# Early units of u beside the selection and between the expert matrix's steps, with the one-hot weights on ScalarE

## The reference, cut to what matters

```python
q = (xb @ w_q).reshape(tb, 8, 2, 128)
s = einsum('thpd,hpnd->thpn', q, sub_keys)          # 128 scores for each half key
sv, si = top_k(s, 16)
cand = (sv[:, :, 0, :, None] + sv[:, :, 1, None, :]).reshape(tb, 8, 256)
top_v, top_i = top_k(cand, 16)
experts = take_along_axis(cand_idx, top_i, -1)      # cand_idx = si[half 0] * 128 + si[half 1]
g = softmax(top_v)
a = gelu(einsum('td,thkd->thk', xb, u[experts]))
y = einsum('thk,thkd->td', g * a, v[experts])
```

## Time and profile before

| | |
|---|---|
| median of 3 runs | 1603.01 us (1602.9 to 1603.34) |
| profiled execution | 1604.01 us, its span 1602.2 us |
| mean granted TensorE clock | 0.953 |
| busy | PE 1429.9 us (89%), PEld 1287.4 (80%), DVE 939.9 (59%), ACT 711.7 (44%), POOL 564.4 (35%) |
| HBM | 259.85 MB read, 4.46 MB written |

### The profile page before, as it was taken

One profiled execution on the slowest core, in us unless ns is written; L12 is line 12 of the kernel. 1 busy time (PEld: TensorE's weight loads), 2 busy tenths in 40 slices (PEclk: granted clock), 3 DMA queues, 4 the chain that ended last, 5 costly groups with the idle time before them and its releaser, 6 DMA issues.

```text
span 1602.2 us, 21914 instructions
## 1 busy us (share of the span) xinstructions
PE 1429.9 (89%) x8932; PEld 1287.4 (80%) x8932; DVE 939.9 (59%) x1493; ACT 711.7 (44%) x991; POOL 564.4 (35%) x314
## 2 busy tenths in 40 slices
PE   6878878999997987977467799999999999999997
PEld 6767767999886766877466688999999999999996
DVE  4786677544455565799788655544444444444444
ACT  4544444544444454432222344544444444444442
POOL 2661012444354103677588721221212222121222
PEclk9999879999999999989788899999999999999999
DMA  8564335777774614534200066666555655555554
GB/s 269 157 187 128 110 116 189 250 234 247 238 242 135 204 59 134 173 95 142 82 1 1 21 201 196 209 190 191 185 188 190 188 186 188 191 185 188 191 187 171
DMA packets 183124, 265.74 MB, mean 166 GB/s; under 512 B 8384, under 2 KB 119744, under 8 KB 182768
## 3 DMA queue, kind: packets, MB, share of 16 engines
q1 hardware_dynamic: 182048, 261.47, 50.8%
q0 software_dynamic: 400, 1.25, 0.3%
q10 hardware_dynamic: 576, 1.63, 0.3%
HBM read 259.85 MB, written 4.46 MB: 165 GB/s over the span
## 4 chain that ended last, share of the span: by engine, by line
PE 70%; DVE 14%; POOL 7%; issue 3%; DMA 3%; ACT 2%; SPq 0%; DVEq 0%; POOLq 0%; ACTq 0%
PE bank L614 21%; PE bank L645 17%; PE bank L619 10%; PE bank L650 8%; POOL sb_hot L1951 5%; PE bank L587 4%; PE bank L591 2%; DVE sb_ada_junk L1260 2%; DMA sb_raw<-w_in 2%; PE bank L890 2%; DVE sb_hot L1761 1%; DVE sb_lo L1244 1%; PE bank L829 1%; PE bank L732 1%; PE bank L848 1%
## 5 line engine op out<-in xcount | busy, mean ns | idle before, releaser
L1812 POOL TENSOR_TENSOR sb_lo<-sb_raw,sb_hi 128x1024 fp32r<-128x1024 f32 (+1 forms) x152 | 373.9, 2467 | 904.3 <-ACT sb_hi L922 904.3
L922 ACT ACTIVATE sb_hi<-sb_raw 128x1024 fp32r<-128x1024 f32 (+2 forms) x427 | 444.5, 1048 | 402.0 <-DMA sb_raw<-peer_v 128.7
L1244 DVE TENSOR_TENSOR sb_lo<-sb_raw,sb_hi 128x1024 fp32r<-128x1024 f32 (+2 forms) x276 | 361.7, 1316 | 412.4 <-ACT sb_hi L922 411.8
L614 PE MATMUL bank<-sb_act_hi,sb_hi 128*128 128x256 f32 x1632 | 410.0, 288 | 5.2 <-ACT sb_hi L922 5.2
L614 PE MATMUL bank<-sb_act_lo,sb_hi 128*128 128x256 f32 x1632 | 407.1, 286 | 0.0
L614 PEld LDWEIGHTS bank<-sb_act_hi,sb_hi 128*128 128x128 f32 x1632 | 318.2, 195 | 9.1 <-issue 4.8
L614 PEld LDWEIGHTS bank<-sb_act_lo,sb_hi 128*128 128x128 f32 x1632 | 318.5, 195 | 2.7 <-issue 0.2
L619 PE MATMUL bank<-sb_act_hi,sb_lo 128*128 128x256 f32 x1632 | 233.0, 286 | 21.0 <-POOL sb_lo L1812 21.0
L645 PE MATMUL bank<-sb_hi,sb_hid_lo 128*128 128x512 f32 x600 | 234.3, 391 | 0.0
L645 PE MATMUL bank<-sb_hi,sb_hid_hi 128*128 128x512 f32 x600 | 234.1, 390 | 0.0
L619 PEld LDWEIGHTS bank<-sb_act_hi,sb_lo 128*128 128x128 f32 x1632 | 213.9, 195 | 22.4 <-POOL sb_lo L1812 22.4
(11 more groups left out here) (317 smaller groups left out, 1467.6 us busy)
## 6 DMA issues: line engine op xcount, KB each, us to landing
sb_raw<-peer_uT SPq DMA_DIRECT2D x128, 512.0 KB, 3.7
sb_raw<-peer_v SPq DMA_DIRECT2D x128, 512.0 KB, 3.6
sb_raw<-w_in SPq DMA_DIRECT2D x52, 512.0 KB, 4.4
sb_ada_w<-ada_wT SPq DMA_DIRECT2D x48, 512.0 KB, 5.0
sb_raw<-w_gate SPq DMA_DIRECT2D x22, 512.0 KB, 3.9
sb_raw<-w_up SPq DMA_DIRECT2D x22, 512.0 KB, 4.1
sb_raw<-w_down SPq DMA_DIRECT2D x22, 512.0 KB, 3.9
sb_raw<-w_out SPq DMA_DIRECT2D x16, 512.0 KB, 4.4
```

What stands on the lines that cost most here:

```text
L614: e.matmul(bank[:, j * T:(j + 1) * T], hi[:, k, j * P:(j + 1) * P], part[:, k0 + k, :], start=i == first_i and j == 0 and k == 0 and part ...
L922: e.activation(flat_of(i, "hi"), flat_of(i, "raw"), ACT.Copy).then_inc(hi_done[i % R], 1)
L1244: e.tensor_tensor(flat_of(i, "lo"), flat_of(i, "raw"), flat_of(i, "hi").bitcast(F32), ALU.subtract).then_inc(lo_done[i % R], 1)
L1812: e.tensor_tensor(flat_of(i, "lo"), flat_of(i, "raw"), flat_of(i, "hi").bitcast(F32), ALU.subtract).then_inc(lo_done[i % R], 1)
```

## The change

1. The selection computes 13 early units instead of 7 (`EARLY_BESIDE_SELECT`), in a new order. GpSimd's two small operations of a D are put off until the lo parts of the H or E that follows are done.
2. 19 further units (`EARLY_BESIDE_G`) are computed between the 64 steps of the expert matrix: `expert_matrix_order` gives one block of u, then one or two steps of G, 38 and 64 in all. Their lo parts are shared in halves by GpSimd and VectorE (`early_G=2`); VectorE is one block ahead with them, not three. So 32 units are early, and the sweep has 32 pairs: one unit of u and two of v.
3. The multiply by the weights leaves GpSimd. ScalarE does it as four `Copy` activations of 128x128 with the token's weight as scale. Its copies into G and its Gelus run five entries of the order later (`G_LATER`).
4. The store of an early unit is issued by ScalarE, right behind the Gelu, not by SyncE. The 19 units of the expert matrix use one more buffer, a fourth.

```diff
-SELECT_ORDER = "HDHHDHDHHDHDHEDEDEEDEDEE"
+SELECT_ORDER = "HDHHDHHDHHDHDEEDEEEDEEEDEEDEEE"
+EARLY_BESIDE_G = 19
+EARLY_BESIDE_SELECT = SELECT_ORDER.count("E")
+EARLY = EARLY_BESIDE_SELECT + EARLY_BESIDE_G
+HOT_BUFS = 3
+G_LATER = 5
+def expert_matrix_order():
+    n_blocks, q = 2 * EARLY_BESIDE_G, 0
+    for b in range(n_blocks):
+        yield "u", EARLY_BESIDE_SELECT + b // 2, b % 2
+        while q * n_blocks < (b + 1) * N_G:
+            yield "G", q, 0
+            q += 1
...
 # TensorE
-            for q in range(N_G):
-                bank = take("G", q)
-                pe.wait_ge(*hot_done.at(q))
+            for what, n, b in expert_matrix_order():
+                if what == "u":
+                    if b == 0:
+                        early_panel = feature_panel(("uT", n), act_T, h2)
+                    next(early_panel, None)
+                else:
+                    bank, h = take("G", n), hot[n % HOT_BUFS]
+                    pe.wait_ge(*hot_done.at(n))
...
 # ScalarE
+            def early_out(u):
+                b, nth = early_slot(u)
+                act.wait_ge(early_stored[b], 16 * nth)
+                act.wait_ge(*full(("uT", u)))
+                e.activation(by_chunk(early_buf[b]), by_chunk(psum(("uT", u))[:, :]), ACT.Gelu).then_inc(*gives(("uT", u)))
+                act.wait_ge(*freed(("uT", u)))
+                e.dma_start(parked_units[u], early_buf[b]).then_inc(early_stored[b], 16)
...
+            order = list(expert_matrix_order())
+            for at in range(len(order) + G_LATER):
+                if at < len(order) and order[at][0] == "u":
+                    hi_until(("uT", order[at][1]), order[at][2])
+                elif at < len(order):
+                    q = order[at][1]
+                    act.wait_ge(*hot_eq.at(q))
+                    for j in range(TG):
+                        h = hot[q % HOT_BUFS][:, 1, j, :]
+                        ins = e.activation(h, h, ACT.Copy, scale=pT[:, 2, q * TG + j:q * TG + j + 1])
+                    ins.then_inc(*hot_done.inc(q))
+                if at >= G_LATER:
+                    what, n, b = order[at - G_LATER]
+                    if what == "G":
+                        copy_out(Gv[:, :, n * TG:(n + 1) * TG], psum("G", n)[:, :].rearrange("p (t i) -> p i t", t=TG), "G", n)
+                    elif b == 1:
+                        early_out(n)
...
 # VectorE
+            for what, n, b in expert_matrix_order():
+                if what == "u":
+                    lo_until(("uT", n), b, 1)
+                else:
+                    h = hot[n % HOT_BUFS]
+                    if n >= HOT_BUFS:
+                        dve.wait_ge(*full("G", n - HOT_BUFS))
...
 # GpSimd
-            for q in range(N_G):
-                pool.wait_ge(*hot_eq.at(q))
-                h = hot[q % HID_BUFS][:, 1]
-                e.tensor_tensor(h, h, pT[:, 2, q * TG:(q + 1) * TG].unsqueeze(2).to_broadcast([P, TG, P]), ALU.mult).then_inc(*hot_done.inc(q))
+            for what, n, b in expert_matrix_order():
+                if what == "u":
+                    lo_until(("uT", n), b)
```

More of the change, by code:

```diff
@@ L67 @@
 SLOT = 2 * BLOCK
[L69 removed]
+POOL_SHARE = dict(early=1, early_G=2, ctx_in2=1, w_gate=2, w_up=2, down=2, wq=1)
 AHEAD = 3
@@ L296, in build @@
                 n_split += 1
-                share = POOL_SHARE.get("early" if b.key[0] == "uT" and b.key[1] < EARLY else b.key[0], 4)
-                lo_on_pool[i] = n_split % share == 0
+                kind = b.key[0]
+                if kind == "uT" and b.key[1] < EARLY:
+                    kind = "early" if b.key[1] < EARLY_BESIDE_SELECT else "early_G"
+                share = POOL_SHARE.get(kind, 4)
+                lo_on_pool[i] = share > 0 and n_split % share == 0
         def flat_of(i, what):
@@ L394, in build @@
         ada_in = [sem(f"ada{i}_in") for i in range(ADA_FIRST_BUFS + ADA_BUFS)]
-        early_stored = [sem(f"early{i}_stored") for i in range(3)]
+        early_stored = [sem(f"early{i}_stored") for i in range(4)]
         hid_in = [sem(f"hid{i}_in") for i in range(HID_BUFS)]
@@ L509, in build @@
         pT = pick_T.rearrange("p (w t) -> p w t", w=3)
-        TG = 4
-        N_G = T // TG
-        hot = [place(f"hot{i}", 1024, F32, OFF["hid"] + 1024 * i).rearrange("p (w t n) -> p w t n", w=2, n=P) for i in range(HID_BUFS)]
+        hot = [place(f"hot{i}", 1024, F32, OFF["hid"] + 1024 * i).rearrange("p (w t n) -> p w t n", w=2, n=P) for i in range(HOT_BUFS)]
         end_i, end_g2_i, end_g_i = span["end_x",][0], span["end_g2",][0], span["end_g",][0]
@@ L885, in tensor_program @@
                 give("picks", t)
-            for q in range(N_G):
-                bank = take("G", q)
-                pe.wait_ge(*hot_done.at(q))
[L889 to L892, removed]
+            early_panel = None
+            for what, n, b in expert_matrix_order():
[7 more added lines that the diff above has]
+                    for j in range(TG):
+                        ins = e.matmul(bank[:, j * P:(j + 1) * P], h[:, 1, j, :], h[:, 0, j, :], start=True, stop=True)
+                    ins.then_inc(*fills("G", n))
+                    give("G", n)
             for b in range(4):
@@ L1183, in scalar_program @@
                     hi_until(("uT", n_e))
[L1184 to L1187, removed]
+                    early_out(n_e)
                     n_e += 1
@@ L1232, in vector_program, with lo_until @@
             let_go = set()
-            def lo_until(key, n=None):
-                end = min(span[key][-1 if n is None else n] + AHEAD, len(plan) - 1)
+            def lo_until(key, n=None, ahead=AHEAD):
+                end = min(span[key][-1 if n is None else n] + ahead, len(plan) - 1)
                 while done_lo[0] <= end:
@@ L1936, in pool_program @@
                 else:
[L1937 to L1946, removed]
-                    n_d += 1
-            for q in range(N_G):
-                pool.wait_ge(*hot_eq.at(q))
-                h = hot[q % HID_BUFS][:, 1]
-                e.tensor_tensor(h, h, pT[:, 2, q * TG:(q + 1) * TG].unsqueeze(2).to_broadcast([P, TG, P]), ALU.mult).then_inc(*hot_done.inc(q))
+                    asked.append(n_d)
+                    n_d += 1
+                    continue
+                while asked:
+                    pairs_and_places(asked.pop(0))
+            for what, n, b in expert_matrix_order():
+                if what == "u":
+                    lo_until(("uT", n), b)
             for at in range(N_UNITS + V_LAG):
```

45 lines of the change are left out of this document (30 added, 15 removed).

## The result

The changed kernel takes 1509.45 us (median of 4, 1507.56 to 1512.89), the kernel before 1602.97 us on the same chip: ratio 0.9419, interval 0.9401 to 0.9436. The forecast was 1518, the range 1499 to 1546. The profiled execution took 1512.9 us, its span 1511.1, against 1604.0 and 1602.2.

What follows compares the result with a forecast made beforehand. PE was taken to bound the sweep, GpSimd's multiply the G stage, VectorE's top-16 chain the selection. 1604.0 - 144.0 + 7 + 52 = 1519.0, less 1.0 for the median: 1518 us, range 1499 to 1546.

Steps and rivals of the forecast that it cites:

- Sweep, -144.0: Sweep: 25 units of u leave it at 5.76 us each, -144.0 us; the 25 reloads in their place cost nothing.
- Selection, +7: Selection: 6 more units lengthen it by 7 us, bounds -2 to +14, with the last block's lo ending it.
- VectorE's 14.1: Selection, three units in a row: GpSimd owes 18 us against VectorE's 14.1 us for a head.
- G stage, +52: G stage: with 19 units and the multiply on ScalarE it takes 184 us instead of 132.1, +52 us.
- the coupling of 6%: G stage: 6% added to the larger engine sum, because two equally loaded engines with short buffers lose something.
- The clock: G stage: PE counted at full clock; had 0.83 stayed, the stage would be about 212 us.
- 2 (PE alone bounds the G stage): G stage 172.5 to 176 us without coupling loss, selection +0 to +4; 1499 to 1508 us; chance 0.14.
- rival 3: Selection: GpSimd sets it, its order behind VectorE's compares; +15 to +25, 1526 to 1536 us; chance 0.07.
- The sign that I gave for rival 3: Selection: PE waits for GpSimd's lo parts beyond 5 us in all.
- Rival 1: G stage: ScalarE bounds it, scalings at 0.40 us without overlap; stage 200 to 222, total 1534 to 1556 us; chance 0.20.
- The multiply's rule cited there: G stage: the Trainium skill puts multiplies on VectorE, not ScalarE; by that, 58 us instead of 77.
- Rival 4: G stage: three one-hot buffers make compare, scaling and matmul run in series; stage 352 us, total 1687; chance 0.04.

Runs made afterwards that it cites:

- e6: The changed kernel with ScalarE's copies and Gelus one entry of the G stage's order later instead of five; 1535.7 us, ratio 0.9580.
- e2: The changed kernel with no units of u between the G steps instead of 19; 1559.8 us, ratio 0.9734.
- e12: The changed kernel with all lo parts of the selection's 13 early units on VectorE; 1523.2 us (one run).

## Why the prediction was right, and where it was off

The direction, the main mechanism (PE's work leaves the sweep and fills the gaps of the two stages before it) and the range held. That the sum comes as near as 9 us to the measured time is luck in part, since its two errors have opposite signs. Of the sum's terms:

- *Sweep, -144.0*: -144.5. The 25 reloads cost nothing.
- *Selection, +7*: +16.1, outside its own bounds of -2 to +14. The step that failed is "VectorE's 14.1": I let VectorE's heads stay 14.1 us apart while GpSimd had 18 us to do, and looked for the cost in late products and late lo parts. Three heads in a row are 19.0 us apart, by the compare's places in the changed kernel's chain of waits (start, length):

```profile
731.62 1.23 DVE sb_eq L1763
...
750.60 1.23 DVE sb_eq L1763
...
769.57 1.24 DVE sb_eq L1763
```

  The end of the path was right: the landing, hi and lo of the last block, the sums and the transposes take 11.7 us behind unit 11, forecast 12.4. But unit 11 is done at 785.6, not 776.5. By my figures VectorE reached the exponential at 771.7 and the end of the last compares at 774, "and this isn't last"; in the trace it reaches the exponential at 779.7, and ScalarE, which works in order and has unit 11's hi part behind the exponential, stands 7.9 us waiting for it. So VectorE's lateness passes to PE by a link that the forecast left out.

  The row that would have told of the long operations was in the trace: a cast of 64 columns with a mean of 1.74 us (L1700), when the smallest takes 0.20. I had taken such durations as fixed, and they are GpSimd's. PE idles 20 us in the selection, of which 8.9 are waiting for GpSimd's lo parts.
- *G stage, +52*: +38.2. Two sizes were wrong. PE's own sum is 109.4 + 64 x 0.895 = 166.7, not 172.5: inside a dense stream a G step takes 0.895 us, and 0.97 was read from the weight loads of steps that stand behind a pause. And the coupling of 6%, 11.5 us, is not there; transposes to sweep is that sum and 3.8 us, 2 of them the first block at the lower clock. e6 shows that the lead of five entries prevents it.
- *ScalarE*: the scaling, which no row showed, was priced at 0.40 us, and at 0.30 overlapped; it is 0.391, and four in a row take 1.17 of e2's chain, so 0.29 each. The Trainium skill ("ScalarE: Activation LUTs", What ACT_TABLE_LOAD costs) gives 186 ns + 93 for a pointer operand + 0.833 per column, by which this form is estimated at 386 ns, and an overlap of 93; the trace agrees, with 391 and about 98.
- *The clock*: 0.99 in the stage. Full, as I had counted on, not the 0.83 of the earlier trace rows.

The two errors, 9.1 too little and 13.8 too much, partly cancel; with 1.4 in the parts before and after they make the 6 us between 1519.0 and the profiled 1512.9.

Of the rivals, 2 (PE alone bounds the G stage) is what happened there, with the selection of rival 3 in size (+16.1 in its +15 to +25). The sign that I gave for rival 3, PE waiting more than 5 us for GpSimd's lo parts, came true with 8.9 us, but it tells nothing: the kernel before has 17.8 us of the same wait. GpSimd's load is behind it, as rival 3 has it, but not by its order behind VectorE's compares (its waits for them fell from 25.6 to 14.4 us): it acts inside VectorE's small instructions. Rival 1 needed PE to wait for scalings; it does for 0.7 us. The multiply's rule cited there, VectorE instead of ScalarE, wasn't tried. Rival 4's series of compare, scaling and passes was not seen even in e6.

## What to carry to other kernels

Work of the bounding engine costs less in stages where it idles, until the stage is full: here 19 units filled one to 99.5%, for 3.3 us each instead of 5.76, and 25.5 us of that hang on the helper engine starting on its next entries before it takes up the results of the last five. Before filling a third engine's gaps, look for tiny instructions of its neighbour with long means: 64 columns at 1.7 us is a wait and not a cost, and it grows with the neighbour's load. When such a wait is removed from one instruction, measure the chain and not the instruction: it moves to the next. And in the list of an engine that works in order, look for an instruction that waits on a slow chain and stands in front of work for the bounding engine, as the exponential does here.

## What the runs showed of the hardware

- VectorE's casts, shifts and compares of two SBUF operands end with GpSimd's running instruction: shifts of 32 columns between 0.17 and 2.45 us; a cast of 64 columns between 0.20 and 2.28. Written as a reduction, the cast takes 0.219 to 0.222.
- It works both ways: GpSimd's product of places rises from a mean of 2.41 to 3.05 us in e12, where VectorE has more to do.
- The eight passes of a G step on PE add 0.89 to 0.90 us to its chain between blocks of u, and 1.13 after a pause, both at full clock.
